# Token norms of a three-layer block on one core: the root taken by eps add, GpSimd power and identity matmuls in place of ScalarE Sqrt and VectorE reciprocal

## What is computed

```
def rms_norm(x, g):
    xf = x.astype(jnp.float32)
    y = xf * lax.rsqrt(jnp.mean(xf * xf, axis=-1, keepdims=True) + EPS)
    return (y * g.astype(jnp.float32)).astype(x.dtype)
...
        u = rms_norm(h, attn_pre_norm[i])
...
        h = h + rms_norm(mix, attn_post_norm[i])
        f = rms_norm(h, ffn_pre_norm[i])
        f = (jax.nn.silu(f @ w_gate[i]) * (f @ w_up[i])) @ w_down[i]
        h = h + rms_norm(f, ffn_post_norm[i])
...
        hres = hres + _rmsnorm(m, norm_g[i, 1])
        h = _rmsnorm(hres, norm_g[i, 2])
        hres = hres + _rmsnorm(_sqrelu_mlp(h, w_up[i], w_down[i]), norm_g[i, 3])
```

## Time and profile before

| | us |
|---|---|
| median of 3 runs | 2229.35 |
| lowest, highest | 2227.07, 2232.45 |
| span of the profiled execution | 2229.9 |
| TensorE busy | 2037.1 (91%) |
| VectorE busy | 1124.7 (50%) |
| ScalarE busy | 695.5 (31%) |
| GpSimd busy | 156.4 (7%) |
| matmuls of the products from z (L278 to L280) | 736.5 + 730.1 + 727.3 |
| matmuls of the products from the arena (L278 to L280) | 397.0 + 396.5 + 394.7 |
| `w_lo` (L260), 152 times | 348.3 |
| six reciprocals of the token norms (L337) | 20.4 |

### The profile page before, as it was taken

The page is one execution under the profiler, slowest core; times in us unless marked ns, Lnnn a source line. Parts: engine busy times, 40 slices in busy tenths (PEclk is TensorE's granted clock), DMA queues, the critical chain, the costliest instruction groups (busy, mean ns, idle before and its releaser), DMA issues.

```text
span 2229.9 us, 28113 instructions
## 1 busy us (share of the span) xinstructions
PE 2037.1 (91%) x11658; PEld 1775.9 (80%) x11658; DVE 1124.7 (50%) x1636; ACT 695.5 (31%) x1003; POOL 156.4 (7%) x123
## 2 busy tenths in 40 slices
PE   7889797999999998888878799999979988999996
PEld 5678675888888787877858799999969976888885
DVE  7573736434434666656563734343375537343343
ACT  4443424222223343333332323122332224232231
POOL 3000004000000220000002200000020022000002
PEclk9996898999999997987869899999989999999998
DMA  4120111222222210101102122222212222222221
GB/s 161 57 94 20 48 39 38 101 108 82 107 84 106 95 60 36 57 20 39 57 0 76 51 95 82 95 94 93 95 38 95 95 76 71 100 95 91 97 92 40
DMA packets 25908, 166.09 MB, mean 74 GB/s; under 512 B 3792, under 2 KB 4048, under 8 KB 6352
## 3 DMA queue, kind: packets, MB, share of 16 engines
q1 hardware_dynamic: 25808, 164.66, 20.9%
HBM read 162.55 MB, written 2.10 MB: 74 GB/s over the span
## 4 chain that ended last, share of the span: by engine, by line
PE 82%; DVE 12%; ACT 3%; issue 1%; POOL 1%; DMA 0%; POOLq 0%; SPq 0%; ACTq 0%; DVEq 0%
PE ps L278 24%; PE ps L279 24%; PE ps L280 24%; PE ps L1414 3%; DVE h L417 2%; PE ps L1416 2%; PE ps L1415 2%; DVE w_lo L260 1%; DVE acc L414 1%; DVE z_lo L369 1%; DVE sq L1275 1%; POOL ssum L353 1%; ACT w_hi L249 1%; PE ps L314 1%; PE ps L307 1%
## 5 line engine op out<-in xcount | busy, mean ns | idle before, releaser
L278 PE MATMUL ps<-z_hi,w_hi 128*128 128x264 f32 (+1 forms) x2192 | 736.5, 336 | 83.2 <-DVE z_lo L369 57.5
L279 PE MATMUL ps<-z_lo,w_hi 128*128 128x264 f32 (+1 forms) x2192 | 730.1, 333 | 0.0
L280 PE MATMUL ps<-z_hi,w_lo 128*128 128x264 f32 (+1 forms) x2192 | 727.3, 332 | 0.0
L278 PEld LDWEIGHTS ps<-z_hi,w_hi 128*128 128x128 f32 x2192 | 418.5, 191 | 143.3 <-issue 37.5
L280 PEld LDWEIGHTS ps<-z_hi,w_lo 128*128 128x128 f32 x2192 | 417.7, 191 | 41.2
L279 PEld LDWEIGHTS ps<-z_lo,w_hi 128*128 128x128 f32 x2192 | 418.2, 191 | 38.5
L249 ACT ACTIVATE w_hi<-w_raw 128x2048 fp32r<-128x2048 f32 x152 | 289.8, 1906 | 436.9 <-PE ps L280 430.6
L260 DVE TENSOR_TENSOR w_lo<-w_raw,w_hi 128x2048 fp32r<-128x2048 f32 x152 | 348.3, 2291 | 148.7 <-ACT w_hi L249 148.7
L278 PE MATMUL ps<-arena,w_hi 128*128 128x264 f32 (+1 forms) x1176 | 397.0, 338 | 14.0 <-DVE arena L1283 8.5
L279 PE MATMUL ps<-arena,w_hi 128*128 128x264 f32 (+1 forms) x1176 | 396.5, 337 | 0.0
L280 PE MATMUL ps<-arena,w_lo 128*128 128x264 f32 (+1 forms) x1176 | 394.7, 336 | 0.0
(11 more groups left out here) (244 smaller groups left out, 1665.4 us busy)
## 6 DMA issues: line engine op xcount, KB each, us to landing
w_raw<-wstream SPq DMA_DIRECT2D x152, 1024.0 KB, 4.8
h<-xT SPq DMA_DIRECT2D x8, 256.0 KB, 6.9
out<-h SPq DMA_DIRECT2D x8, 256.0 KB, 2.0
rope_cs<-pT SPq DMA_DIRECT2D x1, 512.0 KB, 5.5
acc<-pos SPq DMA_DIRECT2D x1, 256.0 KB, 2.7
acc<-lam SPq DMA_DIRECT2D x1, 128.0 KB, 8.8
sm<-small SPq DMA_DIRECT2D x1, 86.0 KB, 2.5
h<-metaT SPq DMA_DIRECT2D x1, 64.0 KB, 9.1
```

The lines of the kernel that those rows point to most:

```text
L278: pe.matmul(dst, wh, zh, start=(k == 0), stop=False)
L279: pe.matmul(dst, wh, zl, start=False, stop=False)
L280: last = pe.matmul(dst, wl, zh, start=False, stop=(k == nk - 1))
```

## The change

All twelve norms take the column form, and the root and the inverse become one power of -0.5:

- `pe_norm` replaces `pe_stat` and `pe_post_stat`. TensorE sums by columns against `mean_w` (a column of 1/1024), waits for `rooted`, and spreads the factors by the identity.
- `dve_mean`: VectorE adds eps to the 4 or 6 columns, out of PSUM into `cols`.
- `pool_root`: GpSimd raises these to -0.5 (`tensor_tensor` with `root_w`, a tile of -0.5). It stands in GpSimd's queue right behind the eight adds of its norm.
- Before a product, ScalarE copies the spread factors from PSUM to `rr` (`act_rstd`), and both TensorE's next block and VectorE's reads wait for that copy (`rstd`). After a product VectorE reads the spread factors in PSUM, as before.
- ScalarE's Sqrt of the norms is gone, with the table loads ahead of it after products (`act_load(act, ACT.Sqrt)`), and so are the reciprocals.
- `pe_stat` with its matmuls against a full matrix of ones, `ones_r` and one memset go.

```
-        def pe_stat(pe, si, slot, ntok, c0):
-            pe.wait_ge(summed, 8 * (si + 1))
-            if ntok <= 512:
-                pe.matmul(ps[:, 4 * slot, 0:ntok], ones[:, :], ssum[:, c0:c0 + ntok], start=True, stop=True).then_inc(stat, 1)
...
-        def pe_post_stat(pe, pi, ntok, c0):
...
-            pe.wait_ge(rstd, si + 1)
+        def pe_norm(pe, si, bank, ntok, c0):
+
+            pe.wait_ge(summed, 8 * (si + 1))
+            pe_columns(pe, ps[:, bank + 2, :], [ssum[:, c0:c0 + ntok]], ntok, by=mean_w[:, 0:1]).then_inc(stat, 1)
+            pe.wait_ge(rooted, si + 1)
+            pe_spread(pe, bank, cols[:, R_COL:R_COL + 6], ntok).then_inc(spread, 1)
+
+        def dve_mean(dve, si, bank, ntok):
+
+            n = len(starts(ntok))
+            dve.wait_ge(stat, si + 1)
+            dve.tensor_scalar(cols[:, E_COL:E_COL + n], ps[:, bank + 2, 0:n], EPS, None, ALU.add).then_inc(mean, 1)
+
+        def pool_root(pool, si, ntok):
+
+            n = len(starts(ntok))
+            pool.wait_ge(mean, si + 1)
+            pool.tensor_tensor(cols[:, R_COL:R_COL + n], cols[:, E_COL:E_COL + n], root_w[:, 0:n], ALU.pow).then_inc(rooted, 1)
...
-        def act_root(act, si, slot, ntok, c0):
-            act.wait_ge(stat, si + 1)
-            act.activation(like(dst, ntok), banks(slot, 0, ntok), ACT.Sqrt, bias=eps[:, 0:1], scale=1.0 / D).then_inc(rooted, 1)
-
-        def dve_rstd(dve, si, ntok, c0):
-            dve.wait_ge(rooted, si + 1)
-            dve.reciprocal(dst, dst).then_inc(rstd, 1)
+        def act_rstd(act, si, bank, ntok, c0):
+            act.wait_ge(spread, si + 1)
+            act.activation(like(dst, ntok), spread_of(bank, ntok), ACT.Copy).then_inc(rstd, 1)
...
+            pool_root(pool, si, ntok)
...
-                if k == KD - 1:
-                    act_load(act, ACT.Sqrt)
...
-            act.wait_ge(stat, si + 1)
-            act.activation(cols[:, R_COL:R_COL + n], ps[:, post_banks(pi, ntok)[1], 0:n], ACT.Sqrt, bias=eps[:, 0:1],
-                           scale=1.0 / D).then_inc(rooted, 1)
...
-            dve.wait_ge(rooted, si + 1)
-            dve.reciprocal(cols[:, R_COL:R_COL + n], cols[:, R_COL:R_COL + n]).then_inc(rstd, 1)
-            dve.wait_ge(s("spread"), pi + 1)
+            dve_mean(dve, si, bank, ntok)
+            dve.wait_ge(spread, si + 1)
...
             def stat_after(b, si, ntok, c0):
-                pe_stat(pe, si, (pair_of(b) + 1) % 2, ntok, c0)
-                pe.wait_ge(rooted, si + 1)
+                pe_norm(pe, si, 4 * ((pair_of(b) + 1) % 2), ntok, c0)
+                pe.wait_ge(rstd, si // 2 + 1)
```

More of the change, by code:

```diff
@@ L94, in build @@
         ones = sb("ones", [P, P])
[L95 removed]
+        mean_w = sb("mean_w", [P, 1])
+        root_w = sb("root_w", [P, 8])
         sm = sb("sm", [P, NSMALL])
@@ L187, in build @@
         zhi, zlo = sem("zhi"), sem("zlo")
-        squared, summed, stat, rooted, rstd = sem("squared"), sem("summed"), sem("stat"), sem("rooted"), sem("rstd")
+        squared, summed, stat, mean, rooted = sem("squared"), sem("summed"), sem("stat"), sem("mean"), sem("rooted")
+        spread, rstd = sem("spread"), sem("rstd")
         scaled, resid = sem("scaled"), sem("resid")
@@ L285, in z_part, with pe_columns @@
             return (z_hi if part == 0 else z_lo)[:, k, :]
-        def pe_stat(pe, si, slot, ntok, c0):
-            pe.wait_ge(summed, 8 * (si + 1))
-            if ntok <= 512:
-                pe.matmul(ps[:, 4 * slot, 0:ntok], ones[:, :], ssum[:, c0:c0 + ntok], start=True, stop=True).then_inc(stat, 1)
-            else:
-                for c in range(2):
-                    last = pe.matmul(ps[:, 4 * slot + c, 0:HALF], ones[:, :], ssum[:, c * HALF:(c + 1) * HALF], start=True, stop=True)
-                last.then_inc(stat, 1)
         def starts(ntok):
             return [P * i for i in range(4)] if ntok <= 512 else [b + a for b in (0, HALF) for a in (0, P, HALF - P)]
-        R_COL = 105
-        def pe_columns(pe, dst, srcs, ntok, step=1):
+        R_COL, E_COL = 105, 113
+        def pe_columns(pe, dst, srcs, ntok, step=1, by=None):
             for i, a in enumerate(starts(ntok)):
                 for k, src in enumerate(srcs):
-                    last = pe.matmul(dst[:, step * i:step * i + 1], src[:, a:a + P], ones[:, 0:1], start=(k == 0), stop=(k == len(srcs) - 1))
+                    last = pe.matmul(dst[:, step * i:step * i + 1], src[:, a:a + P], ones[:, 0:1] if by is None else by, start=(k == 0), stop=(k == len(srcs) - 1))
             return last
@@ L385, in act_post @@
                 between()
-            act.wait_ge(stat, si + 1)
-            n = len(starts(ntok))
-            act.activation(cols[:, R_COL:R_COL + n], ps[:, post_banks(pi, ntok)[1], 0:n], ACT.Sqrt, bias=eps[:, 0:1],
-                           scale=1.0 / D).then_inc(rooted, 1)
             if pi == 5:
@@ L404, in dve_post @@
             si = 2 * pi + 1
-            n = len(starts(ntok))
-            bank = post_banks(pi, ntok)[0]
-            roots = ps[:, bank, 0:S] if ntok <= 512 else ps[:, bank:bank + 2, 0:HALF]
-            dve.wait_ge(rooted, si + 1)
-            dve.reciprocal(cols[:, R_COL:R_COL + n], cols[:, R_COL:R_COL + n]).then_inc(rstd, 1)
-            dve.wait_ge(s("spread"), pi + 1)
+            bank = post_bank(pi, ntok)
+            roots = spread_of(bank, ntok)
+            dve_mean(dve, si, bank, ntok)
+            dve.wait_ge(spread, si + 1)
             for k in range(KD + 1):
```

62 lines of the change are left out of this document (29 added, 33 removed).

## The result

| | us |
|---|---|
| after, median of 4 runs | 2277.43 (2271.41 to 2283.64) |
| before, median of 4 runs beside them | 2228.21 |
| ratio, 95% interval | 1.022 (1.0196 to 1.0243) |
| after in a second series, median of 4 | 2271.35 (2268.07 to 2275.64), ratio 1.0195 (1.0177 to 1.0213) |
| span of the profiled executions | 2273.4 and 2269.5; before 2229.9 |

The kernel became slower by about 2%. The forecast was 2256.2 with a range of 2246 to 2272. The sign was right; the added time was 42 to 49 us where 26.8 was forecast, and both the first series and the median of all eight lie above the range; only the second series lies inside it, by 0.65 us.

A forecast was written before the change was run, and what follows sets the result against it. TensorE was taken as the bound, with 82% of the chain that ended last. Terms 9.7 + 3.8 + 8.5 + 1.4 + 3.4 = 26.8 us on the 2229.9 span gave 2256.7, median about 2256.2 us, range 2246 to 2272.

The forecast's parts named there:

- The sign: Whole kernel: slower, with chance 0.94, against 0.03 for faster and 0.03 for the same.
- The path: All twelve norms: every delay of TensorE at a norm is carried to the end of the kernel.
- The rival by which norm 0's delay is made good later: Convolution and mLSTM stages: their waits absorb norm 0's 9.7 us, giving 2246.5 us; 9 in 100.
- the two in which the clock gives it all back: Whole kernel: faster through the clock, near 2222, 3 in 100; or nothing changes, 2229, 2 in 100.
- Norm 0: First norm: block 1 starts at 37.15, 7.9 us late, behind VectorE's queued add; with slow clock, 9.7 us lost.
- The power's price x: GpSimd's power at each norm: taken at 0.6 us, range 0.10 to 1.26.
- 1.31 + x: Norms 2 and 10, 512 tokens before a product: growth of TensorE's stop, 1.9 us each, 3.8 together.
- 2.2 + x: Norm 4, 528 tokens before a product: loss of 2.8 us; norms 4, 6 and 8 together 8.5 us.
- The rival of a slow power: GpSimd at all norms: element by element, x of 2.5 us or more, giving 2279; 13 in 100.
- the first call that pays 6 us: Norm 0's power on GpSimd: a first-call cost would end norm 0 6 us later, 2262; no chance given.
- The clock: Five later norms before a product: two extra clock drops in five, 3.4 us, range 0 to 5.
- After a product: Norms 1, 3, 5, 7, 9, 11: six times 0.34 us, minus 0.6 at norm 1, plus 1.4 us.

The follow-up runs named there:

- e_early: The changed kernel with VectorE's add of eps at norm 0 moved ahead of the second set of rotary angles: 2267.42 us.
- e_shift: The kernel before with four filler matmuls of 512 columns between norm 0 and block 1: 2232.45 us, ratio 1.0012.
- e_pre: The changed kernel with the six norms after a product back in the old form: 2262.38 us, ratio 1.0152.
- e_fill: The changed kernel with unread filler matmuls on TensorE behind the columns of all norms and behind the spread of the norms before a product: 2263.87 us.
- e_combo: The changed kernel with both the edit of e_early and the fillers of e_fill: 2261.75 us.
- e_wait: The kernel before with TensorE waiting for VectorE's reciprocal in place of ScalarE's root at the six norms before a product: 2260.71 us, ratio 1.0154.
- e_post: The kernel before with only the six norms after a product in the new form: 2234.47 us, ratio 1.0026.

## Why the prediction was off

**The path, right.** A delay at a norm goes to the end: 5.5 us less of stop at norm 0, with less slow clock behind it, gave 5.9 us (e_early), and the stretch behind norm 0 took 321.2 to 322.5 us in seven kernels whose stop there was 0.8 to 9.9 us; e_shift's 3.0 us fit too, though with a wide interval. The rival by which norm 0's delay is made good later is out, and so are the two in which the clock gives it all back.

**Norm 0, right.** Block 1 was forecast at 37.15 and came at 36.37, with the add at 32.28 instead of 33.5, the power 0.43 us longer than taken and the first matmul 0.64 us earlier. The spread took the 2.08 us taken for it, and the clock was at 0.50 from 32 to 41: from block 1's start at 36.37 to 42 it was 0.53, some 2.6 us lost where 2.0 was taken. (Those 2.0 came from 3.9 us at norm 1; by the earlier trace rows it is 4.3, since 0.55 in the slice at 363 leaves the clock low until 363.9.)

**The power's price x, mis-sized: the first step that failed.** It was taken at 0.6 us, near the middle between a memset of 0.10 and an add of 512 elements of 1.26, "since neither row is near in kind". It is 1.02 for 4 columns, and 1.33 for 6, the latter over the upper end of 1.26. With x = 1.02 the formula 1.31 + x gives 2.33 us for norms 2 and 10, where the first trace has 2.35 at both (the second has 4.0 at norm 2, by the slow spread and the late add above); with 1.33, 2.2 + x is 3.5 for norm 4, where the traces have 3.7 and 3.5. So the steps of these sums hold and the one term was too small: 7 x 0.42 + 5 x 0.73 = 6.6 us over all norms. The rival of a slow power, x of 2.5 or more, is out too. So is the first call that pays 6 us: the first power, at norm 0, took 1.03 us against a mean of 1.019 (1.28 at most, in e_early).

**The clock, mis-sized: the second step that failed.** "I take two drops in five" met five in five, in both traces. Their cost: the work behind norms 2, 6, 8 and 10 lost 1.5 + 2.5 + 1.8 + 1.6 = 7.5 us, and at norms 6 and 8 the spread itself ran slow (2.93 and 2.80 us, where it takes 1.60 at full clock in e_pre), 2.5 more; what norm 4's drop cost lies in attention and can't be read. That makes 10 us against 3.4; in the second trace it is 8 (4.6 in the work, 0.9 + 1.3 + 1.3 in slow spreads). Five in five isn't a rule, as e_pre and the others show, and no run tells which stops bring a fall. e_fill shows the cause: with TensorE kept busy the same norms have a clock of 1.00 (with one exception, norm 8 of e_combo). e_wait shows that nothing of the new form is needed for it, only a longer wait.

**After a product, too small.** Forecast 1.4 us, measured 5.7 (e_post; its interval is 2 to 9). Between columns and spread the six norms pay 0.79, 0.63, 1.09, 1.09, 0.78 and 0.78 us, not 0.34 each, and the longer power makes up nearly all of the difference; at norm 1 the table load's absence gives back 0.42, not 0.6 (4.12 to 3.70). That sums to 4.7.

**Sum.** 26.8 + 6.6 for the power + 5 to 7 for the clock gives 38 to 40, and the runs have 43.9. So neither failed step alone carries the time past 2272, and the two together do not reach it either: 2256.2 + 12 to 14 is 2268 to 2270. What took the median to 2273 is the 4 to 6 us that remain. They are of the size by which attention, norm 4 to norm 5, differs between two traces of one kernel (404.02 and 407.87), and stay unassigned. Chance isn't shown for them either: the six traces with the old form at norm 4 have 395.7 to 401.7 there, the eight with the new form 397.2 to 407.9.

## What to carry to other kernels

Ask of each norm or reduction between products not how many instructions it has but for how long the matmul engine has nothing queued: the same operations cost 27 us less in the medians (15 to 18 of them found at those norms by the traces) when they wrote to a bank that the next block didn't need, and a wait on a later partner at six norms cost 32 us by itself. A short operation on the critical path whose price no row shows deserves a generous upper bound: the middle between unlike rows was too low by 0.4 to 0.7 us at each of twelve norms, and the bound of 1.26 was too low for 6 columns. And count the clock with every new stop, including the stops that the kernel has already: filling them gave 7.5 us.
